# A seam between two blocks: the keys' normalisation applied behind the projections, and rows added by column blocks

## The reference

```python
    x = x + hierarchical_moe(rms_norm(x, ffn_norm[l]), ...)      # end of first_block
    return rms_norm(x, final_norm)                               # y = x * rsqrt(mean(x*x) + EPS) * final_norm
...
    # hybrid_layer, the second block, on h = that result
    xn = rmsnorm(x, norm_mix)
    (u_rnn, u_gate, q, k_c, v_c, k_s, v_s, k_w, v_w, g_nsa, g_a, g_b) = jnp.split(xn @ w_in, cuts, axis=-1)
    ...
    kc = rmsnorm(compress_blocks(kv(k_c), phi_k_pe, phi_k_w1, phi_k_w2), kc_norm)
    vc = compress_blocks(kv(v_c), phi_v_pe, phi_v_w1, phi_v_w2)
    h = x + merged @ w_out
```

## Time and profile before

| what | value |
|---|---|
| median of 3 runs | 1241.64 us (1238.59 to 1244.49) |
| the profiled execution, its own time | 1243.32 us |
| its span in the trace | 1241.5 us |
| busy, share of the span | PE 97%, PEld 86%, DVE 73%, ACT 58%, POOL 9% |
| granted TensorE clock, mean | 0.99 |

### The profile page before, as it was taken

How to read it: one execution, slowest core, us unless ns; L and a number is a source line. 1 busy time by engine, 2 the same in 40 slices (tenths; PEclk the granted TensorE clock), 3 DMA queues, 4 the chain that set the end, 5 groups by cost and what they waited for, 6 DMA issues and landing times.

```text
span 1241.5 us, 18815 instructions
## 1 busy us (share of the span) xinstructions
PE 1203.7 (97%) x7842; PEld 1069.0 (86%) x7842; DVE 900.7 (73%) x960; ACT 723.0 (58%) x839; POOL 117.9 (9%) x137
## 2 busy tenths in 40 slices
PE   6999999999999999999999899999999999999998
PEld 6978997978888787888877788999999998989897
DVE  5897586557778878888889884758766875755554
ACT  4855224454577677776767454667778744544432
POOL 0100000000000000000000100019732520000000
PEclk8999999999999999999999999989999999999999
DMA  7433234515489888898998156533234446455552
GB/s 269 170 128 144 103 127 144 192 68 212 163 325 369 336 322 340 319 366 313 341 340 335 73 179 239 198 105 103 84 122 162 149 136 220 157 196 201 179 197 102
DMA packets 38179, 255.43 MB, mean 206 GB/s; under 512 B 4192, under 2 KB 6368, under 8 KB 10320
## 3 DMA queue, kind: packets, MB, share of 16 engines
q1 hardware_dynamic: 34800, 247.64, 55.2%
q10 hardware_dynamic: 3296, 6.61, 1.5%
HBM read 253.15 MB, written 1.08 MB: 205 GB/s over the span
## 4 chain that ended last, share of the span: by engine, by line
PE 76%; DVE 11%; ACT 7%; issue 3%; POOL 2%; DMA 1%; DVEq 0%; SPq 0%; ACTq 0%; POOLq 0%
PE bank L447 21%; PE bank L449 21%; PE bank L448 21%; DVE r L1795 4%; ACT r L1226 3%; PE bank L457 2%; PE bank L848 1%; PE bank L612 1%; PE bank L1090 1%; POOL f L2639 1%; PE bank L814 1%; PE bank L672 1%; PE bank L711 1%; DVE r L1804 1%; DMA f<-in_weights 1%
## 5 line engine op out<-in xcount | busy, mean ns | idle before, releaser
L1795 DVE TENSOR_TENSOR r<-f,r 128x2048 fp32r<-128x2048 f32 (+2 forms) x239 | 540.9, 2268 | 176.1 <-ACT r L1226 175.7
L447 PE MATMUL bank<-r,r 128*128 128x256 f32 (+5 forms) x1936 | 644.3, 333 | 12.8 <-DVE r L1795 5.8
L449 PE MATMUL bank<-r,r 128*128 128x256 f32 (+5 forms) x1936 | 633.7, 327 | 0.0
L448 PE MATMUL bank<-r,r 128*128 128x256 f32 (+5 forms) x1936 | 633.3, 327 | 0.0
L1226 ACT ACTIVATE r<-f 128x2048 fp32r<-128x2048 f32 (+3 forms) x240 | 453.3, 1891 | 171.6 <-PE bank L449 146.1
L447 PEld LDWEIGHTS bank<-r,r 128*128 128x128 f32 (+4 forms) x1936 | 359.4, 186 | 57.3 <-issue 18.1
L449 PEld LDWEIGHTS bank<-r,r 128*128 128x128 f32 (+4 forms) x1936 | 359.4, 186 | 34.6
L448 PEld LDWEIGHTS bank<-r,r 128*128 128x128 f32 (+4 forms) x1936 | 359.2, 186 | 34.5 <-issue 1.0
L1804 DVE TENSOR_TENSOR r<-f,r 128x512 fp32r<-128x512 f32 (+3 forms) x70 | 52.8, 764 | 30.5 <-ACT r L1762 11.2
L2639 POOL TENSOR_SCALAR f<-f,f 128x128 f32<-128x128 f32 (+1 forms) x64 | 63.8, 1013 | 44.6 <-DVE f L2425 44.6
L457 PE MATMUL bank<-f,f 128*128 128x128 f32 x224 | 32.1, 303 | 8.4 <-DMA f<-in_cst 6.3
(11 more groups left out here) (325 smaller groups left out, 1075.3 us busy)
## 6 DMA issues: line engine op xcount, KB each, us to landing
f<-in_weights SPq DMA_DIRECT2D x216, 1024.0 KB, 4.9
f<-in_weights SPq DMA_DIRECT2D x12, 896.0 KB, 4.7
f<-in_weights SPq DMA_DIRECT2D x8, 672.0 KB, 4.6
f<-in_weights SPq DMA_DIRECT2D x4, 882.0 KB, 5.4
f<-bias_table ACTq DMA_DIRECT2D x1, 2048.0 KB, 13.0
f<-in_mem ACTq DMA_DIRECT2D x1, 1024.0 KB, 4.7
out<-f ACTq DMA_DIRECT2D x2, 512.0 KB, 2.6
f<-in_moe ACTq DMA_DIRECT2D x1, 647.0 KB, 4.7
```

Source lines behind the costliest of these rows:

```text
L447: e.matmul(o, lh.r, rh.r, start=start, stop=False)
L448: e.matmul(o, lh.r, rl.r, start=False, stop=False)
L449: return e.matmul(o, ll.r, rh.r, start=False, stop=stop)
L1795: e.tensor_tensor(slot_of(n).r, slot_of(n).f, high_of(n).r.bitcast(F32), ALU.subtract).then_inc(s["w_lo"], 1)
```

## The change

It touches the seam only, except that the quarters of all the additions to X are now taken in the order 0, 2, 1, 3 (both row halves of the first 512 columns, then those of the second), as the first and the last addition had it.

- Keys' copy, q = 4: its row scales are left out ahead of the projections. The transposed quarters, with gains alone, are split and projected. For k_c and v_c the scales are multiplied on at the head of `blocks` (a row of 256 scales, copied from a bank to `SCR`), whose result goes through the buffer `KDD`; for k_s, v_s, k_w and v_w ScalarE multiplies by a column of scales (`rcol`) when it reads the banks. `rcol` comes out of two more matmuls of one column.
- TensorE turns q = 4 and q = 5 of each quarter one behind the other. Both scale rows (bank of q = 4 and of q = 5) stand behind the first half of ksvs.
- The splitting of q = 4 begins when the first two quarters are there; the low part of kcvc 1 (the "final weights"), the products with `final_norm`, their squares and GpSimd's roots come behind it.
- The work on the weights of ksvs to q2a is set at other places of the two lists.

```diff
@@ -256,6 +256,7 @@
         OT, OTH = (room2(2048).re("p (c t) -> p c t", c=8) for _ in range(2))
+        rcol = small(2)
         xmx, xsm, xri, xsc = small(8), small(8), small(8), small(2)
@@ -292,6 +293,7 @@
         KDD = at_word(area0 + 1024, 2048).f
+        SCR = KDD[:, 1024:1280]
         BLH = at_word(area0 + 3072, 1920)
@@ -368,20 +370,16 @@
         SCALES = [0, 2, 4, 6, 8, 12]
...
         ORDER = (0, 2, 1, 3)
-        LATE = (2, 6)
+        LATE = (2, 4, 6)
         DIAGONALS = {q: 2 * n for n, q in enumerate((0, 1, 3, 4, 5))}
-        SCALED = {q: 4 * n for n, q in enumerate((0, 1, 3, 4, 5))}
...
-        def order_of(call):
...
-            return ORDER if call in (0, OUT2) else (0, 1, 2, 3)
+        SCALED = {q: 4 * n for n, q in enumerate((0, 1, 3, 5))}
...
-            return 4 * call + order_of(call).index(a) + 1
+            return 4 * call + ORDER.index(a) + 1
@@ -469,8 +467,10 @@
                     m = e.matmul(banks[b][:, i * 128:(i + 1) * 128], C("ones"), dg[2 * (q % 2) + i], start=True, stop=True)
+                    if q == 4:
+                        m = e.matmul(banks[b][:, 256 + i:257 + i], dg[2 * (q % 2) + i], C("ones")[:, 0:1], start=True, stop=True)
                 full["row", q] = done(m)
-                freed[b] = ("n_mu", SCALED[q] + 4)
+                freed[b] = ("ev_d", READ_AT["kcvc", 1]) if q == 4 else ("n_mu", SCALED[q] + 4)
@@ -549,7 +549,7 @@
                     wh, wl = high_of(n).re("p (k f) -> p k f", k=2), slot_of(n).re("p (k f) -> p k f", k=2)
-                    for a in order_of(call):
+                    for a in ORDER:
                         i, f = a // 2, slice((a % 2) * 512, (a % 2) * 512 + 512)
@@ -915,16 +915,13 @@
-            for a in range(4):
+            for a in ORDER:
                 turn_added(4, OUT2 - 1, a)
-            scale_row(4)
-            for a in range(4):
                 turn(5, a)
...
                 proj_t("kcvc", 1, c, 8, 128, XRR, "ev_d")
-            scale_row(5)
             for name in ("ksvs", "kwvw", "q2a", "q2b"):
@@ -936,6 +933,9 @@
                         proj_r(name, 0, u, i, XTT if name in ("q2a", "q2b") else XRR)
+                    if name == "ksvs" and u == 0:
+                        scale_row(4)
+                        scale_row(5)
             b = take("gn")
@@ -1231,7 +1231,7 @@
                 i, hf = a // 2, a % 2
-                number = SUMS[r] + (2 * a + n if r == 4 else ORDER.index(a) if r in (2, 5) else a)
+                number = SUMS[r] + (ORDER.index(a) + 4 * n if r == 4 else ORDER.index(a) if r in (2, 5) else a)
                 if number >= 2:
@@ -1490,12 +1490,10 @@
-            for a in range(4):
-                e.wait_ge(s["x_add"], added(OUT2 - 1, a))
-                square(4, X, a)
-                e.wait_ge(s["xf"], a + 1)
+            high_and_square(4, 4, OUT2 - 1)
+            for a in ORDER:
+                e.wait_ge(s["xf"], ORDER.index(a) + 1)
                 square(4, XF, a, 1)
-            turn_high(4)
             e.dma_start(PCC[0:32, 0:1024], bcon).then_inc(s["l_b"], 16)
@@ -1504,16 +1502,16 @@
             ahead(("kcvc", 1))
+            ahead(("ksvs", 0))
             block_high(0)
-            ahead(("ksvs", 0))
+            ahead(("ksvs", 1))
             turn_high(5)
-            ahead(("ksvs", 1))
-            block_high(1)
             for name in ("ksvs", "kwvw", "q2a", "q2b"):
...
                 if name == "kwvw":
+                    block_high(1)
                     e.wait_ge(s["bi_t"], 1)
@@ -1527,8 +1525,9 @@
                         w = int(name == "kwvw")
-                        e.activation(QKv[:, i, 16 + 4 * w:20 + 4 * w, :], o[:, 0:256].rearrange("p (g d) -> p g d", g=4), ACT.Copy)
-                        m = e.activation(VS[:, i, w, :], o[:, 256:512], ACT.Copy)
+                        e.wait_ge(s["ev_d"], READ_AT["kcvc", 0])
+                        e.activation(QKv[:, i, 16 + 4 * w:20 + 4 * w, :], o[:, 0:256].rearrange("p (g d) -> p g d", g=4), ACT.Copy, scale=rcol[:, i:i + 1])
+                        m = e.activation(VS[:, i, w, :], o[:, 256:512], ACT.Copy, scale=rcol[:, i:i + 1])
                     else:
@@ -1872,7 +1871,7 @@
-            def add_back(call, last, scale=None, quarters=range(4)):
+            def add_back(call, last, scale=None, quarters=ORDER):
                 for a in quarters:
@@ -2228,7 +2227,7 @@
-            def spread(g, quarters=range(4)):
+            def spread(g, quarters):
                 for a in quarters:
@@ -2278,42 +2277,48 @@
                 if x_ >= 5 and x_ % 4 == 1:
-                    spread(g - 1, range(2))
+                    spread(g - 1, ORDER[0:2])
                 hidden(x_)
...
                     if x_ >= 5 and x_ % 4 == 1:
-                        spread(g - 1, [2])
+                        spread(g - 1, ORDER[2:3])
                     ahead(("down", 2 * x_ - 1))
                     if x_ >= 5 and x_ % 4 == 1:
-                        spread(g - 1, [3])
+                        spread(g - 1, ORDER[3:4])
             hidden_low(EXPERTS - 1)
...
             outcome_low(TILES - 1)
+            last = TILES - 1
+            spread(last, ORDER[0:2])
+            spread_gain(4, 0)
+            spread(last, ORDER[2:3])
+            spread_gain(4, 2)
+            spread(last, ORDER[3:4])
+            turn_low(4, 0)
+            turn_low(4, 1)
+            spread_gain(4, 1)
+            spread_gain(4, 3)
+            turn_low(4, 2)
+            turn_low(4, 3)
...
             ahead(("down", 2 * EXPERTS - 1))
             e.wait_ge(s["l_f"], 16)
-            for a in range(4):
-                spread(TILES - 1, [a])
+            for a in ORDER:
                 xf = XF[:, a // 2, (a % 2) * 512:(a % 2 + 1) * 512]
...
                 e.tensor_tensor(xf, X[:, a // 2, (a % 2) * 512:(a % 2 + 1) * 512], FB[:, (a % 2) * 512:(a % 2 + 1) * 512], ALU.mult).then_inc(s["xf"], 1)
...
-            for a in range(4):
-                spread_gain(4, a)
-            diagonal(4, 0)
-            diagonal(4, 1)
-            normalise(4)
             for a in range(4):
                 spread_gain(5, a)
-            for i in range(2):
-                diagonal(5, i)
...
                 wait_unit(("kcvc", p))
-                o = banks[bank_at["kcvc", p]][:, :].rearrange("p (j t) -> p j t", j=2)
+                o = KDD[:, 512 * p:512 * p + 512].rearrange("p (j t) -> p j t", j=2)
+                after(own(e.tensor_tensor(o, banks[bank_at["kcvc", p]][:, :].rearrange("p (j t) -> p j t", j=2),
+                                          SCR.unsqueeze(1).to_broadcast([128, 2, 256]), ALU.mult)))
                 for g in range(4):
@@ -2329,25 +2334,33 @@
             ahead(("kcvc", 0))
+            for q in (4, 5):
+                for i in range(2):
+                    diagonal(q, i)
+            ahead(("kcvc", 1))
+            e.wait_ge(s["pe_done"], full["row", 4])
+            e.tensor_copy(rcol, banks[bank_at["row", 4]][:, 256:258])
+            after(own(e.tensor_copy(SCR, banks[bank_at["row", 4]][:, 0:256])))
             blocks(0)
-            ahead(("kcvc", 1))
+            ahead(("ksvs", 0))
             block_low(0)
-            ahead(("ksvs", 0))
+            ahead(("ksvs", 1))
             normalise(5)
-            ahead(("ksvs", 1))
+            ahead(("kwvw", 0))
             blocks(1)
...
             for name in ("kwvw", "q2a", "q2b"):
-                ahead((name, 0))
+                if name != "kwvw":
+                    ahead((name, 0))
                 ahead((name, 1))
...
                         cols = (slice(None), a // 2, slice((a % 2) * 512, (a % 2 + 1) * 512))
-                        e.wait_ge(s["xf"], a + 1)
+                        e.wait_ge(s["xf"], ORDER.index(a) + 1)
                         e.tensor_scalar(X[cols], XF[cols], rows[4][a // 2][4], None, ALU.mult).then_inc(s["x4"], 1)
@@ -2599,15 +2612,17 @@
                     t = rows[r][i]
-                    e.wait_ge(s["n_sq"], SUMS[r] + 4 * i + 3)
+                    first, second = (SUMS[r] + ORDER.index(2 * i + hf) + 1 for hf in range(2))
+                    e.wait_ge(s["n_sq"], second)
                     k = own(e.tensor_scalar(t[4], t[0], t[1], None, ALU.add))
...
                     e.wait_ge(s["c_pool"], k)
+                    e.wait_ge(s["n_sq"], 4 + first)
                     k = own(e.tensor_scalar(t[5], t[5], t[2], None, ALU.add))
-                    e.wait_ge(s["n_sq"], SUMS[r] + 4 * i + 4)
+                    e.wait_ge(s["n_sq"], 4 + second)
                     e.wait_ge(s["c_pool"], k)```

```

(1 more changed line is left out.)

## The result

The changed kernel takes 1246.79 us, the median of 22 runs (1244.41 to 1250.41); the kernel before, on the same chip, 1242.79 us (22 runs, 1237.47 to 1246.12). The ratio is 1.0035, with a 95% interval of 1.0025 to 1.0046. By the bound of 0.5% that is no change, though the interval leaves no doubt of the sign: 4 us slower. The forecast was 1246.1 us. The profiled execution took 1247.02 us for a span of 1245.1.

A forecast was written before the change was run, and what follows sets the result against it. PE, busy 97% of the span, was taken to bound the kernel. Later q2a +1.95, clock +1.7, table overlap +0.6 and third norm +0.2 gave +4.45 us on the median 1241.64: 1246.1 us, range 1240.5 to 1250.5.

The forecast's parts named there:

- the seam's wait and slow clock: Before the first scale row: PE's 2.69 us wait and the slow clock behind it, costing 1.7 us, would both go.
- q2a's wait for the bank of kcvc 1: At q2a: PE stands 6.9 us until VectorE's second additions end, so q2a starts 1.95 us later than before.
- The waits: At the seam: new PE waits of 1.65 us before kcvc 1, about 1.05 before kwvw and 6.9 before q2a.
- the rival of a fall at kcvc 1: Clock falls already at kcvc 1 if its wait reaches 2.2 us: +6.7 us, 1248.3 us; chance 0.17.
- the wait's length decides: At kcvc 1: a wait nearer 2.69 than 1.77 us, so 2.2 or more, makes the clock fall, adding 1.7 us.
- The 16 additions: Behind the scale row, from the buffer: 3.9 us as from the bank, at most 0.6 us more per `blocks`.
- The clock: Behind q2a's wait: granted clock falls as it did at the seam, +1.7 us, bounds 0 to 2.
- The bias table's load: Before w1: longer overlap of this load with a weight transfer lengthens the wait at 788.07, +0.6 us, bounds 0 to 1.0.
- The third norm: Near 284 us: quarter 1's square waits for the third addition instead of the second, +0.2 us, bounds 0 to 0.6.
- The sum: Whole kernel: q2a +1.95, clock +1.7, table +0.6, third norm +0.2, together +4.45 us, giving 1246.1 us; chance 0.62.
- The rule on fixed costs: VectorE additions of both `blocks`: 62 cycles less each from the buffer, 2.1 us for 32; the prediction's rows contradicted it.
- The rule of the same page on different quadrants: VectorE additions: inputs on different quadrants lose overlap with earlier instructions, 0.6 us per `blocks` if all 16 lose it.

The follow-up runs named there:

- gains5: Changed kernel with the four spreadings of the final gain ahead of the second block's products; median 3.5 us over again.
- quad: Changed kernel, small additions reading position vectors from the partitions of their other input, values partly wrong; profiled execution 1245.49 us, ratio of four runs not used.
- inplace: Changed kernel, the multiplication writing back into its bank and the 16 additions reading the bank; median 3.55 us lower than again.
- again 2: Changed kernel, unchanged, repeated as control on a third chip; median 1245.99 us.
- again: Changed kernel, unchanged, run once more with a profile; 5.7 us over the kernel before, profiled span 1248.3 us.
- fill: Changed kernel plus 26 matmuls into a bank nobody reads during PE's wait ahead of q2a; median 0.8 us lower than again, five runs.
- blocks first: Changed kernel, second multiplication and its additions ahead of the low part of q2a's first weights; ratios to the kernel before 1.0041 and 1.0024 in two sets.
- free: Changed kernel, both multiplications early and releasing the banks, additions behind the weights' work; medians 4.4 and 6.1 us under the kernel before, 1236.16 us in the second set.

## Why the prediction was right, and where it wasn't

The time was right (1246.1 forecast, 1246.79 measured), and so was the mechanism: the seam's wait and slow clock go, and q2a's wait for the bank of kcvc 1 takes back more than they were worth. Three sizes were off, and the last two of them, clock and table, cancelled (+0.6, -0.6). That the forecast of +4.45 us fits a measured +4.0 to +5.1 is partly luck: at w1 the loss is 7.0 us where 4.25 were forecast, and what brings it back lies in stretches of which the forecast said nothing.

- *The waits.* Forecast 1.65, 1.05 and 6.9 us; measured 1.44, 2.06 and 6.39, each ended by the instruction named. "Clock 1.00 through kcvc 0" holds, so the rival of a fall at kcvc 1 is out: the wait stayed under its 2.2 us. Its rule, that the wait's length decides, fails all the same: behind a wait of 2.50 us in gains5 the clock stayed at 1.00, behind 2.06 us and, in quad, 1.68 us at kwvw it fell.
- *The 16 additions* are the term that was mis-sized. Taken at 3.9 us with 0.6 more at most (4.6 to 5.3 with the multiplication for the second); measured 5.5. The row on which the price rested was of another shape (128x128, 293 ns) and was read as saying that a buffer costs an addition next to nothing; with 64x120, read with a step of sixteen, it costs 350 ns instead of 277. With ksvs' reads (1.42 us, not 1.05) that puts q2a 4.75 us later than before, not 1.95: from the copies to the weight unit 6.8 us instead of 5.5 (+1.3), from the low part of q2a 0 to the end of the additions 6.1 instead of 5.0 (+1.1), and 0.4 for the reads, 2.8 in all.
- *The clock.* Forecast 1.7 us behind q2a's wait; q2a and q2b took 24.24 us instead of 21.98, so 2.3. A second fall, not forecast, came behind kwvw's wait of 2.06 us: kwvw took 12.9 us (727.55 to 740.4) instead of 11.3. It cost nothing there, since PE had then to wait for VectorE anyway; it is why q2a's wait was 6.4 us and not 8. In inplace, with 0.46 us there, kwvw ran at 1.00.
- *The bias table's load* was priced at +0.6. From gn to w1 it is 23.54 us, as 23.56 before, and w1's wait is 0.95 instead of 1.08: nothing. In again 2 it is 24.11 with a wait of 1.45, so up to 0.5 us in one profile of three.
- *The third norm*, +0.2: from its first transposes to its first projection it is 6.95 us (285.50 to 292.45) instead of 6.71 (284.42 to 291.13): +0.24.
- *The sum.* These give 7.0 us at w1 instead of 4.25. The difference of the means, 5.1, is less, and the profiles show where, on the mean of two of before and three of the changed kernel. To w1 it is 6.9 us more (104.8, 111.7), behind w1 1.2 less (55.2, 54.0), up to the row at 684 1.0 less (684.1, 683.1), behind L1066 0.8 more (397.3, 398.1): together 5.4, which is the difference of their spans (1241.5, 1246.9). The stretches that no edit touches differ by falls of the clock whose place changes. One near 1005 us in again and again 2 (0.91 and 0.83 from 1000 to 1010, 1.00 in the first profile) costs 1.5 us. With so few profiles the 1.0 and the 0.8 are the rest of a sum, and no measured effect of the change.
- *What stays open* is the part that the other runs of fill and blocks first did not return. The 34 runs of the changed kernel lie 6.0 us apart, the 73 of before 8.8, and the former's times go with the mean granted clock of the run (correlation -0.8), so the likeliest place is falls of the clock in other runs than the profiled ones. That is argued, not shown.
- *The rule on fixed costs* from the Trainium skill (VectorE: DVE Perf Modes, The TRN2 errata) would, by the prediction's estimate from its figures, have made 32 additions 2.1 us cheaper out of the buffer. They became 3.1 us dearer: 350 ns against 277. The 128x512 operations show nothing of it either, 682 ns from the bank and 685 from the buffer. The measurement decides against it for both. The rule of the same page on different quadrants (Two Vector instructions with no wait between them), by which such an instruction starts only when the earlier ones have finished, is borne out by quad in kind: a single addition takes 349 ns there and 350 in the changed kernel, but sixteen take 0.4 us less there, where no addition has its inputs on different partitions, as half of the sixteen have in the changed kernel.

## What to carry to other kernels

When a step is moved behind a wait, look at which buffer it holds until it ends: here the additions no longer read the bank but still stood ahead of its release, and releasing it at the multiplication, with the additions moved behind the weights' work, was worth 10 to 11 us and turned a loss of 5 into a gain of 4 to 6. Price an operation with a changed source by a row of its own shape and its own step between elements, or measure it alone; a row of another shape, read as "the same", was the largest error here. And when one execution is compared with one other, measure distances between fixed points of the program first, since a stretch that no edit touches may differ by 3 us through the clock alone.

## What was not expected of the hardware

- A VectorE addition of 64x120 elements, of which the first input is read with a step of sixteen, takes 277 ns with that input in a bank and 350 ns with it in the buffer, where 128x512 without such a step takes 682 and 685 ns. From one start to the next it is 0.244 us from the bank, 0.32 from the buffer on equal partitions, 0.344 with half of them on different ones.
- ScalarE's copy of 128x256 out of a bank takes 0.46 to 0.48 us with a column of scales; without one the row before has 0.36.
- The length of a wait doesn't say whether the clock falls behind it: behind 0.46 (inplace), 1.44, 1.76 and 2.50 us (gains5, 712.1 to 714.6) it stayed at 1.00, behind 1.68 us (quad, 0.57 from 726 to 728.5) and 2.06 us (0.56 from 727.5 to 730) it fell. What PE did ahead differed as well.
- A wait of 6.4 us filled with matmuls that nobody reads kept the clock at 1.00 (0.50 without).
- Between 1060 us and the end the same matmuls at a clock of 1.00 take 178.48 us in both profiles of free and 175.31 to 176.15 in all others; no run shows why.
